# Moving the constants, the arena and the split inputs of a fused two-block decoder kernel to multiples of 1024 bytes in their partition

## The chip, the cores and the metric

The kernel runs on one core of one Trainium2 chip. The metric is the device time of one execution in microseconds (us). A core has TensorE (PE, whose weight loads are shown apart as PEld), VectorE (DVE), ScalarE (ACT), GpSimd (POOL), and SyncE (SP), which here issues all DMAs. Every tensor of the on-chip memory lies in 128 partitions; "the place" of a tensor is the byte in its partition at which it begins, and it is the same in all partitions.

## The reference

Two transformer blocks are applied to 256 tokens of width 1024, all in float32.

```python
def reference(x, mem, positions, ...):
    x = first_block(...)   # h = rms_norm(x); proj = h @ w_in; differential attention, indexed attention,
                           # gated sum @ w_out; memory attention; PEER feed-forward
    return second_block(...)   # layer 0: stick-breaking attention + RWKV7; layer 1: MLA
                               # each with a conv-GLU feed-forward and a gated per-layer embedding
```

In the PEER feed-forward each token picks, by product keys, 16 of 16,384 experts for each of 8 heads. The kernel computes it densely: 128 groups of 128 experts, of which each has a row of `peer_u` and a row of `peer_v`.

## The kernel before

All weights are streamed once through `ring`, four slots of 128 x 1024 float32 (512 KB), in the fixed order of `PLAN`. SP waits until a slot is free (`send`, L405) and issues the next DMA. Each slot is split in two halves of 128 x 512. ACT copies a half to `w_high` in the reduced format float32r (`split_high`, L453), DVE subtracts it from the original and writes the rest to `w_low` (`split_low`, L459), and both have four slots. The inputs of a product are split in the same manner into `a_high` and `a_low` (L1040, L1047, L1142 and L1147). A product of two float32 matrices is then made of three float32r matmuls in `three`:

```python
        (lh, ll), (rh, rl) = pairs
        self.nc.tensor.matmul(to, lh, rh, start=start, stop=False, **more)
        self.nc.tensor.matmul(to, lh, rl, start=False, stop=False, **more)
        return self.nc.tensor.matmul(to, ll, rh, start=False, stop=stop, **more)
```

For most products the weights (128 x 128) are stationary and the split inputs (128 x 256) are moving. These matmuls are L503, L504 and L505. Small products (sums of squares with the constant matrix `ones` at L907, L884 and L511, attention and the recurrence) are plain float32 matmuls; the profiler records each of those as two.

The tensors are laid out one behind the other, in the order in which `Kernel.__init__` (L290) names them; each begins at the next multiple of 32 bytes. Behind them come the tensors of a room (`room`, L321): an `arena` of so many floats, and then `a_high` and `a_low` (`pairs`, L333). A room is opened for a part of the program and closed behind it, and its place is used again. There are four rooms in turn:

- the first mixer, arena of 86 x 256 floats, 16 chunks of split inputs
- `peer` (L1953), arena of 128 x 256 floats. In the place of `a_high` and `a_low` (8 chunks) stand later `hot`, and then `s_high` and `s_low`, the split inputs of the products with `peer_v`
- `hybrid` (L2575), arena of `HYBRID_ROOM` floats, 11 chunks
- the rest of the second block, arena of 70 x 256 floats, 32 chunks

The products of `peer_u` (370 to 715 us) and of `peer_v` (833 to 1183 us) run mostly in a loop whose body handles four groups, so that the same instructions with the same places come round again and again. Semaphores order everything. Nothing in the order of the work depends on a place.

Of the kernel before, what the change touches and what calls it, by code (L numbers as in the profile page):

```python
# [29 lines left out]
P = 128  # L30
T = 256
TT = T // P
# [11 lines left out]
MEM_AT = 76 * T  # L44
POSITIONS_AT = 65 * T
PLE_AT = 30 * T
HYBRID_ROOM = 31488
AHEAD = 3
L = 64
SUB = 16  # L50
# [70 lines left out]
class Counter:  # L121


    def __init__(self, make):
        self.make, self.made, self.base, self.total = make, None, 0, 0
# [164 lines left out]
class Kernel:  # L290
    def __init__(self, nc, ctx, dram, out):
        self.nc, self.ctx, self.dram, self.out = nc, ctx, dram, out
        self.counters = {}
        sb = lambda name, shape, dt=F32: ctx.enter_context(nc.sbuf_tensor(name, shape, dt))
        self.x = sb("x", [P, DC, T])
        self.hn = sb("hn", [P, DC, T])
        self.ring = sb("ring", [P, RING, BLK * P])
        self.w_high = sb("w_high", [P, SLOTS, HALF * P], F32R)
        self.w_low = sb("w_low", [P, SLOTS, HALF * P], F32R)
        self.params = sb("params", [P, N_PARAMS])  # L300
        self.consts = sb("consts", [P, len(CONSTS), P])
        self.side = sb("side", [P, 6 * P])
        self.by_row = sb("by_row", [P, 2 * TT])
        self.small = sb("small", [P, 512])
        self.bank = [ctx.enter_context(nc.psum_tensor(f"bank{i}", [P, 512], F32)) for i in range(8)]
        self.landed = [ctx.enter_context(nc.semaphore(f"weights_landed{i}")) for i in range(RING)]
        self.high = ctx.enter_context(nc.semaphore("weights_high"))
        self.low = ctx.enter_context(nc.semaphore("weights_low"))
        self.used = ctx.enter_context(nc.semaphore("weights_used"))
        self.sent = 0  # L310
        self.split = 0
        self.taken = 0
        self.rooms = 0
        self.chains = {}
        self.x_landed = [ctx.enter_context(nc.semaphore(f"x_landed{i}")) for i in range(4)]
        self.consts_landed = ctx.enter_context(nc.semaphore("consts_landed"))
        self.fetched = Counter(
            lambda: ctx.enter_context(nc.semaphore("fetched")))
# [2259 lines left out]
    def hybrid(self):  # L2578
# [5 lines left out]
        def place(chunks, width=T):  # L2584
            at = free[0]
            free[0] += chunks * width
            assert free[0] <= HYBRID_ROOM - 2 * T
            return self.at(at, chunks, width)
# [772 lines left out]
def build(nc, dram, out):  # L3361
    with ExitStack() as ctx:
# [3 lines left out]
        k.peer()  # L3366
        with k.room(HYBRID_ROOM, DC + 3):
            out = k.hybrid()
# [139 lines left out]
```

How the kernel before makes its waits and increments, by code:

```python
        def link(ins):  # L357
            ins.then_inc(c.up(), 1)
            eng.wait_ge(c.sem, c.total)
# [46 lines left out]
    def send(self, sp, g, at, source, it=0, turn=0):  # L406
        if g >= RING:
            sp.wait_ge(self.low, it * (2 * turn) + 2 * (g - RING + 1))
        if self.wide(g):
            self.send_wide(sp, g, at)
            return
        if self.of("mla_uq", g):
            self.send_heads(sp, g, at)
            return
        sp.dma_start(self.ring[:, at, :], source).then_inc(self.landed[at], 16)
# [29 lines left out]
    def split_high(self, act, h, it=0, turn=0):  # L447
        g = h // 2
        act.wait_ge(self.landed[g % RING], it * (8 * turn // RING) + self.landings(g))
        if h >= SLOTS:
            act.wait_ge(self.used, it * turn + (h - SLOTS + 1))
        self.nc.scalar.activation(self.cut(h, self.w_high), self.raw(h), ACT.Copy)\
            .then_inc(self.high, 1)
# [1 line left out]
    def split_low(self, dve, h, it=0, turn=0):  # L456
        dve.wait_ge(self.high, it * turn + (h + 1))
        self.nc.vector.tensor_tensor(self.cut(h, self.w_low), self.raw(h),
                                     self.cut(h, self.w_high.bitcast(F32)), ALU.subtract)\
            .then_inc(self.low, 1)
# [22 lines left out]
    def block_of(self, pe, n):  # L484
        h = n // HALF
        if n % HALF == 0:
            pe.wait_ge(self.low, h + 1)
        at = slice((n % HALF) * P, (n % HALF + 1) * P)
        return self.w_high[:, h % SLOTS, at], self.w_low[:, h % SLOTS, at]
# [1031 lines left out]
        def bank_free(pe):  # L1522
            pe.wait_ge(kept.sem, kept.at(1))
```

## Time and profile before

| | |
|---|---|
| time, median of three runs | 2025.58 us |
| lowest and highest | 2023.09 and 2032.52 us |
| span of the profiled execution | 2021.6 us |
| PE busy | 1877.1 us, 93% |
| PEld, DVE, ACT busy | 1800.7, 1456.5 and 1242.6 us |
| DMA | 296.06 MB, 146 GB/s over the span |

The profiled execution's own time is known as its span alone; it lies 4.0 us below the median of the runs and 1.5 us below the lowest. The span runs from the first to the last instruction of the program. Busy times are sums over an engine's instructions. Matmuls overlap in the array and each is recorded with its full length, so a PE that is shown busy without a gap may still work at one pace or another; the pace is read from the starts.

### The profile page before, as it was taken

To read this page: it belongs to the slowest core of one execution; us is meant where nothing else is said; L and a number is where in the kernel's file an instruction comes from. 1 tells how busy PE (TensorE), PEld (TensorE's weight loads), DVE (VectorE), ACT (ScalarE), POOL (GpSimd) and SP (SyncE) were. 2 spreads that over 40 slices of the span, in tenths; PEclk is the share of its full clock that TensorE was granted. 3 is DMA by queue.
4 is the path that set the end of the run, shared out by engine and by line. 5 is a ranking of instruction groups with operands and counts; after the bars stand their busy time and mean duration, and the time that the engine had idled before them with its cause. 6 is when DMAs were issued, how large, how long until landed. Compare 5 with 4: busy or idle time off the path is not lost. (4 is left out here: it accounts for less than half of the span.)

```text
span 2021.6 us, 45016 instructions
## 1 busy us (share of the span) xinstructions
PE 1877.1 (93%) x16518; PEld 1800.7 (89%) x16518; DVE 1456.5 (72%) x3046; ACT 1242.6 (61%) x2420; POOL 0.2 (0%) x4
## 2 busy tenths in 40 slices
PE   8998988999999999999999989687999977999997
PEld 8887888999999976899999989587999976899996
DVE  7667667688985479766666667776888678578857
ACT  5454655777776789655555556733665555666555
POOL 0000000000000000000000000000000000000000
PEclk9999999999999999999999999798999989999998
DMA  6533344466655620266666646101665644166562
GB/s 208 158 97 105 118 143 136 132 194 193 179 186 175 186 84 0 84 194 190 196 191 193 193 139 199 52 3 56 184 196 173 192 126 136 34 190 189 176 198 76
DMA packets 102084, 296.06 MB, mean 146 GB/s; under 512 B 9539, under 2 KB 32454, under 8 KB 101830
## 3 DMA queue, kind: packets, MB, share of 16 engines
q1 hardware_dynamic: 101958, 294.35, 47.0%
q8 instruction: 83, 1.36, 0.3%
q14 instruction: 43, 0.35, 0.1%
HBM read 293.26 MB, written 1.05 MB: 146 GB/s over the span
## 5 line engine op out<-in xcount | busy, mean ns | idle before, releaser
L459 DVE TENSOR_TENSOR w_low<-ring,w_high 128x512 fp32r<-128x512 f32 x1102 | 743.2, 685 | 357.1 <-ACT w_high L453 349.2
L503 PE MATMUL bank<-a_high,w_high 128*128 128x256 f32 x3228 | 921.2, 285 | 74.3 <-DVE w_low L459 39.1
L504 PE MATMUL bank<-a_low,w_high 128*128 128x256 f32 x3228 | 907.5, 281 | 0.0
L505 PE MATMUL bank<-a_high,w_low 128*128 128x256 f32 x3228 | 907.4, 281 | 0.0
L453 ACT ACTIVATE w_high<-ring 128x512 fp32r<-128x512 f32 x1102 | 671.4, 624 | 375.3 <-PE bank L505 372.8
L503 PEld LDWEIGHTS bank<-a_high,w_high 128*128 128x128 f32 x3228 | 620.0, 192 | 90.0 <-DVE w_low L459 39.7
L504 PEld LDWEIGHTS bank<-a_low,w_high 128*128 128x128 f32 x3228 | 616.3, 191 | 0.4
L505 PEld LDWEIGHTS bank<-a_high,w_low 128*128 128x128 f32 x3228 | 616.7, 191 | 0.0
L503 PE MATMUL bank<-s_high,w_high 128*128 128x256 f32 x1024 | 283.5, 277 | 2.0 <-DVE s_low L2446 2.0
L504 PE MATMUL bank<-s_low,w_high 128*128 128x256 f32 x1024 | 283.3, 277 | 0.0
L505 PE MATMUL bank<-s_high,w_low 128*128 128x256 f32 x1024 | 283.3, 277 | 0.0
L503 PEld LDWEIGHTS bank<-s_high,w_high 128*128 128x128 f32 x1024 | 192.9, 188 | 2.2 <-DVE s_low L2446 2.2
L504 PEld LDWEIGHTS bank<-s_low,w_high 128*128 128x128 f32 x1024 | 193.0, 188 | 0.0
L505 PEld LDWEIGHTS bank<-s_high,w_low 128*128 128x128 f32 x1024 | 192.9, 188 | 0.0
L2329 PEld LDWEIGHTS bank<-hot 128*128 128x128 f32 x512 | 63.2, 194 | 28.6 <-issue 18.1
L2073 ACT ACTIVATE arena<-bank 128x256 f32 (+1 forms) x128 | 49.1, 384 | 58.0 <-PE bank L505 57.2
L2329 PE MATMUL bank<-hot 128*128 128x128 f32 x512 | 74.4, 290 | 9.8 <-ACT hot L2266 8.7
L1040 ACT ACTIVATE a_high<-x,params 128x256 fp32r<-128x256 f32 x72 | 31.9, 500 | 49.5 <-DVE x L1273 35.0
L2446 DVE TENSOR_TENSOR s_low<-arena,s_high 128x256 fp32r<-128x256 f32 x128 | 53.4, 418 | 0.8 <-ACT s_high L2426 0.8
L2300 DVE TENSOR_SCALAR hot<-consts,hn 128x128 f32<-128x128 f32 x192 | 53.2, 340 | 0.4 <-PEq L2023 0.4
L2426 ACT ACTIVATE s_high<-arena 128x256 fp32r (+1 forms) x128 | 51.5, 403 | 2.7 <-PEq L2243 2.7
L1047 ACT ACTIVATE a_high<-arena 128x256 fp32r<-128x256 f32 x87 | 30.5, 407 | 30.0 <-DVE arena L1333 12.7
(368 smaller groups left out, 1867.8 us busy)
## 6 DMA issues: line engine op xcount, KB each, us to landing
ring<-in_stream SPq DMA_DIRECT2D x273, 512.0 KB, 3.7
ring<-in_peer_u SPq DMA_DIRECT2D x128, 512.0 KB, 3.6
ring<-in_peer_v SPq DMA_DIRECT2D x128, 512.0 KB, 3.5
ring<-in_stream SPq DMA_DIRECT2D x32, 256.0 KB, 3.3
ring<-in_stream SPq DMA_DIRECT2D x12, 192.0 KB, 2.7
x<-in_x SPq DMA_DIRECT2D x4, 256.0 KB, 6.3
arena<-in_mem SPq DMA_DIRECT2D x1, 1024.0 KB, 11.0
out<-x SPq DMA_DIRECT2D x4, 256.0 KB, 2.6
```

What stands on the lines that cost most here:

```text
L453: self.nc.scalar.activation(self.cut(h, self.w_high), self.raw(h), ACT.Copy)\
L459: self.nc.vector.tensor_tensor(self.cut(h, self.w_low), self.raw(h), self.cut(h, self.w_high.bitcast(F32)), ALU.subtract)\
L503: self.nc.tensor.matmul(to, lh, rh, start=start, stop=False, **more)
L504: self.nc.tensor.matmul(to, lh, rl, start=False, stop=False, **more)
L505: return self.nc.tensor.matmul(to, ll, rh, start=False, stop=stop, **more)
L1040: ins = nc.scalar.activation(self.a_high[:, to, :], source.source[:, c, :], ACT.Copy, scale=self.param(source.gain, c))
L1047: ins = nc.scalar.activation(self.a_high[:, to, :], source[:, c, :], ACT.Copy)
L2073: nc.scalar.activation(to, self.bank[k % 4][:, 0:T], ACT.Gelu)\
L2300: ins = nc.vector.tensor_scalar(hot[:, 1, b, i, :], iota, one(1), one(2), ALU.is_equal, ALU.mult)
L2329: ins = nc.tensor.matmul(self.bank[b][:, i * P:(i + 1) * P], hot[:, 0, b, i, :], hot[:, 1, b, i, :], start=True, stop=True)
L2426: nc.scalar.activation(s_high[:, k % SIDES, :], self.arena[:, bass.ds(it * (RING * T) + k * T, T)], ACT.Copy).then_inc(cut[0].sem, 1)
L2446: nc.vector.tensor_tensor(s_low[:, k % SIDES, :], self.arena[:, bass.ds(it * (RING * T) + k * T, T)], s_high[:, k % SIDES, :].bitcast(F32) ...
```

## The change

One tensor is made larger and moved, and one room is made smaller. `by_row` (16 bytes, four per-partition factors) stood between `side` and `small`. It is now the beginning of `filled` (480 bytes), which stands between `params` and `consts`.

```diff
-HYBRID_ROOM = 31488
+HYBRID_ROOM = 31232
...
         self.params = sb("params", [P, N_PARAMS])
+        self.filled = sb("filled", [P, 120])
+        self.by_row = self.filled[:, 0:2 * TT]
         self.consts = sb("consts", [P, len(CONSTS), P])
         self.side = sb("side", [P, 6 * P])
-        self.by_row = sb("by_row", [P, 2 * TT])
         self.small = sb("small", [P, 512])
```

`HYBRID_ROOM` loses 256 floats, 1024 bytes, which makes up for the bytes that the gap adds; what `hybrid` places in it (at most `HYBRID_ROOM - 512` floats, asserted at L2587) still fits, and the last 512 floats of the arena, its `scratch`, move down with its end.

The places of the built programs, in bytes from the start of the partition:

| tensor | before | after | remainder by 1024, before and after |
|---|---|---|---|
| x, hn, ring, w_high, w_low, params | 16512, 24704, 32896, 49280, 57472, 65664 | the same | 128 and 128 |
| consts | 67104 | 67584 | 544 and 0 |
| side | 75296 | 75776 | 544 and 0 |
| small | 78400 | 78848 | 576 and 0 |
| arena, every room | 80448 | 80896 | 576 and 0 |
| a_high, a_low, first room | 168512, 184896 | 168960, 185344 | 576 and 0 |
| a_high, a_low, peer | 211520, 219712 | 211968, 220160 | 576 and 0 |
| hot and s_high; s_low | 211520; 215616 | 211968; 216064 | 576 and 0 |
| a_high, a_low, hybrid | 206400, 217664 | 205824, 217088 | 576 and 0 |
| a_high, a_low, last room | 152128, 184896 | 152576, 185344 | 576 and 0 |

The instructions of every engine and of SP stand in the same order in both programs, with the same shapes, numbers and waits; where the profile will name `by_row` it will name `filled`, and lines behind L301 are one higher.

## Rows read from the trace of the kernel before

**Rows 1.** The page, part 1: busy us (share of the span) and instructions.

```profile
PE 1877.1 (93%) x16518; PEld 1800.7 (89%) x16518; DVE 1456.5 (72%) x3046; ACT 1242.6 (61%) x2420; POOL 0.2 (0%) x4
```

**Rows 2.** Groups by line: busy us, mean ns | idle before, releaser.

```profile
L503 PE MATMUL bank<-a_high,w_high 128*128 128x256 f32 x3228 | 921.2, 285 | 74.3 <-DVE w_low L459 39.1 <-DVE a_low L1147 15.8 <-DVE a_low L1142 10.8
...
L459 DVE TENSOR_TENSOR w_low<-ring,w_high 128x512 fp32r<-128x512 f32 x1088 | 737.9, 688 | 356.0 <-ACT w_high L453 348.3
L453 ACT ACTIVATE w_high<-ring 128x512 fp32r<-128x512 f32 x1088 | 666.3, 627 | 368.7 <-PE bank L505 366.2
...
L505 PE MATMUL bank<-s_high,w_low 128*128 128x256 f32 x1024 | 283.3, 277 | 0.0
```

**Rows 3.** Windows: length; PE, PEld, DVE, ACT, POOL busy (x starts); PEclk, DMA, GB/s.

```profile
370.00:521.00 151.00, 151.00 (x1335) 151.00 (x1334) 130.00 (x435) 117.20 (x195) 0.00 (x0) 1.00 0.63 191
...
838.00:1182.00 344.00, 344.00 (x3038) 344.00 (x3037) 217.00 (x378) 198.14 (x379) 0.00 (x0) 1.00 0.62 192
...
1918.00:1971.00 53.00, 53.00 (x470) 53.00 (x469) 31.52 (x51) 26.68 (x47) 0.00 (x0) 1.00 0.65 197
```

**Rows 4.** Windows of five other stretches, the same columns.

```profile
617.00:649.00 32.00, 32.00 (x273) 32.00 (x273) 15.11 (x25) 20.68 (x38) 0.00 (x0) 1.00 0.59 182
652.00:714.00 62.00, 62.00 (x528) 62.00 (x528) 31.07 (x48) 47.21 (x80) 0.00 (x0) 1.00 0.62 192
1456.00:1550.00 94.00, 94.00 (x801) 94.00 (x799) 77.97 (x144) 57.77 (x107) 0.00 (x0) 1.00 0.62 186
1763.00:1783.00 20.00, 20.00 (x172) 20.00 (x171) 13.44 (x24) 10.45 (x20) 0.00 (x0) 1.00 0.56 173
1806.00:1912.00 106.00, 106.00 (x902) 106.00 (x902) 88.14 (x163) 65.04 (x121) 0.00 (x0) 1.00 0.60 186
```

**Rows 5.** Windows of PE alone: length, busy (x), PEclk, DMA, GB/s.

```profile
233.00:253.00 20.00, 20.00 (x173) 1.00 0.56 171
...
1973.00:1985.00 12.00, 12.00 (x104) 1.00 0.58 176
```

**Rows 6.** Timeline of PE in the peer_u loop at 500 us: start, length.

```profile
500.08 0.28 PE L503 MATMUL bank<-a_high,w_high 128*128 128x256 f32 x1
...
500.42 0.28 PE L503 MATMUL bank<-a_high,w_high 128*128 128x256 f32 x1
```

**Rows 7.** Timeline of PE in the same loop at 680 us.

```profile
679.85 0.28 PE L503 MATMUL bank<-a_high,w_high 128*128 128x256 f32 x1
...
680.20 0.28 PE L503 MATMUL bank<-a_high,w_high 128*128 128x256 f32 x1
```

**Rows 8.** Timeline of PE at 616.7 us, where the pace changes.

```profile
616.81 0.39 PE L503 MATMUL bank<-a_high,w_high 128*128 128x256 f32 x1 [0.67 <-DVE w_low L459]
617.04 0.28 PE L504 MATMUL bank<-a_low,w_high 128*128 128x256 f32 x1
...
617.27 0.28 PE L503 MATMUL bank<-a_high,w_high 128*128 128x256 f32 x1
```

**Rows 9.** Source views of L907, L884 and L511: min/median/max ns, first and last start.

```profile
L907 PE MATMUL bank<-hn,consts x50: 377/379/380, 26.5 to 1987.6; 128*128 128x256 f32 x50
...
L884 PE MATMUL bank<-arena,consts x36: 377/379/380, 33.9 to 87.7; 128*128 128x256 f32 x36
...
L511 PE MATMUL bank<-consts x50: 377/379/634, 295.8 to 1724.0; 128*128 128x256 f32 x50
```

**Rows 10.** Groups by line of DVE: busy us, mean ns | idle before.

```profile
L1171 DVE TENSOR_TENSOR hn<-hn 128x512 f32<-128x512 f32 x28 | 19.2, 684 | 0.0
...
L1207 DVE TENSOR_TENSOR arena<-arena 128x512 f32<-128x512 f32 x11 | 7.6, 692 | 0.4
```

**Rows 11.** DMA issues: count, KB each, median us to landing.

```profile
ring<-in_stream SPq DMA_DIRECT2D x273, 512.0 KB, 3.7
...
arena<-in_mem SPq DMA_DIRECT2D x1, 1024.0 KB, 11.0
```

**Rows 12.** Waits: us, times, longest.

```profile
ACT w_high L453 <- PE bank L505: 372.8, 572, 2.6
...
ACT L1040 <- DMA x<-in_x: 6.8, 1, 6.8
```

## The prediction

> **What bounds the kernel now.** I read the page's busy times first, then the groups by line, then windows of long stretches, and last the starts of single matmuls. PE is busy for 1877.1 of 2021.6 us [rows 1]; POOL does nothing. In the groups, ACT idles 366.2 us before its weight split because it waits for PE to free a slot of the split weights, and DVE idles 348.3 us because it waits for ACT [rows 2]; the list of waits says the same, 572 waits of at most 2.6 us [rows 12]. PE itself idles 74.3 us before L503, the line that starts most products. So PE sets the pace, the splitters wait for it, and the weights' DMAs, 3.7 us to landing [rows 11], are issued when the splitters have freed a slot. Half the time comes from one kind of instruction: L503, L504 and L505 with 128 x 256 moving, 3 x 3228 with `a_` inputs and 3 x 1024 with `s_` inputs, 12,756 in all [rows 2].
>
> The length of a record says little, since matmuls overlap. The pace is what counts, and the reader is to see two paces. In long stretches where PE never pauses and the granted clock is 1.00 (the 2.4 GHz level), 344 us hold 3038 matmuls, 151 us hold 1335 and 53 us hold 470 [rows 3]. A count includes the two that began before the stretch, so the pitch is 344 / 3036 = 113.3 ns, and 113.3 and 113.2 in the others. In seven other stretches, also without a pause and at clock 1.00, the counts are 273 in 32 us, 528 in 62, 801 in 94, 172 in 20 and 902 in 106 [rows 4], and 173 in 20 and 104 in 12 [rows 5]: 346 us for 2939 matmuls, 117.7 ns. Single starts show it too: three matmuls take 0.34 us at 500 us [rows 6] and 0.35 us at 680 us [rows 7], in the same loop with the same tensors in the same places. The slow pace begins where PE restarts after a wait [rows 8] and then lasts for hundreds of matmuls. So for the weight products there is a second, slower pace of the pair "load the next weights, stream the inputs", 4.4 ns per matmul dearer, into which PE falls at some restarts.
>
> **The change part by part.** It adds no instruction, removes none, and moves none in any queue, SP's included. What changes is where tensors begin. Each of its effects is a difference in how long an instruction takes.
>
> (1) The moving operand of the weight products goes from remainder 576 to 0 by 1024, while the stationary weights stay at 128 (or 640, by the 512-byte block). No row of before has `a_high` at another remainder, so I bound it. Nearest is the same 128 x 256 shape with a constant matrix beside it: with `hn`, which begins at remainder 128, L907 takes 377/379/380 ns; with the arena, at 576, L884 takes 377/379/380 ns [rows 9]. Two remainders, no difference in minimum, median or maximum. Those are plain float32 matmuls, whose stationary side is `consts`, but they read on-chip memory in the same shape. I take 0. The bounds from other rows are the two paces: all matmuls of the seven slow stretches at the fast pace gives 2939 x 4.4 ns = 13 us less; all of the three long fast stretches (1333 + 3036 + 468 = 4837) at the slow pace gives 21 us more, and every one of the 12,756 - 2939 = 9817 others gives at most 43 us more, since waits and half-clock stretches hide part of that.
>
> (2) The constants go from remainder 544, which is no multiple of 64, to 0. L511 has constants on both sides and a median of 379 ns, the same as L907 and L884, which have them on one side only [rows 9]. Its maximum of 634 is a matmul at the low clock level or behind a pause. So the price is 0; if the one or two ns that rounding hides were real, 144 records (50 + 36 + 50 and L907's eight others) make under 0.3 us.
>
> (3) DVE and ACT read and write arena, `small` and split inputs. DVE's 128 x 512 addition-like operation takes 684 ns with `hn` (128) on all sides and 692 ns with the arena (576) on all sides [rows 10]; if the arena's remainder were the cause, DVE would gain at most 8 ns on each. Both engines wait for PE, 366.2 and 348.3 us, so this hides, except where DVE's chain between two products holds PE: PE idles 74.3 us before L503 [rows 2], and 8 / 692 of that is 0.9 us. I take 0 and keep -1 us for the range.
>
> (4) `by_row` moves; its four factors per partition are read as scales. Nothing there depends on bulk reads: 0. The 1024 bytes less in `hybrid` leave out unused space: 0.
>
> (5) DMAs. The weights' slots stay at 128 by 1024, so the loads that run all through the kernel land as they did. What changes is the landing of the constants, the memory tokens, keys and a few small loads, once each; the largest takes 11.0 us and lands while PE works, and the first thing on the start's path is the load of `x`, 6.8 us of waiting [rows 11, 12], whose place is unchanged: 0.
>
> The sum is 0 against the profiled span of 2021.6 us. The median of the runs lies 4.0 us above that span, and I forecast it unchanged, **2025.6 us**. The time by itself moves, though: the three runs spread over 9.4 us, and the seven slow stretches show a reason, restarts that fall to one pace or the other. If the restarts fall otherwise in the changed kernel without any cause in the places, a few us either way follow; one long stretch of 106 us changing pace is 902 x 4.4 ns = 4 us. I give that +-8 us. About 10 us (0.5%) is what a measurement of this kernel can tell from no change.
>
> **A rule to weigh.** The rows show one instruction, with one set of places and clock 1.00, at two paces that differ by 3.9% [rows 3, 4]; something that PE reads or shares costs it those 4.4 ns in one state and not in the other. The Trainium skill, page "SBUF — State Buffer", section on the two separate sides, says that on the engine side only the port pair shared by VectorE and GpSimd causes contention, and that TensorE never waits for anyone. By that rule the place can't matter and the sum is exactly 0, with neither of the first two rivals below possible. The two paces don't fit well with it, which is why I keep the rivals.
>
> A second rule speaks for a small gain. The page "DMA: Bandwidth & Descriptors", section on how a descriptor splits, says that a transfer that doesn't start at a multiple of 256 bytes costs one more transaction for each descriptor. By it the 8 KB rows of the memory tokens would need 32 instead of 33, an estimate of 0.3 us on 11.0, beside other work, while the weights' 512 KB slots gain nothing since the change leaves them at 128. The sum by it stays 0.
>
> **The rivals.**
>
> *The slow pace goes away (faster).* The weight load and the moving read may hinder each other depending on the distance of their places. The change makes that distance 896 instead of 448 by 1024. For: two paces exist, one set of places gives both, so the state is a matter of phase, and a distance shifts a phase. Against: within a stretch the weights' remainder alternates between 128 and 640 and the pace doesn't, so 512 bytes of distance are worth nothing; and L907 and L884, whose distances to the constants differ by those same 448 bytes, take the same time [rows 9]. Time: 2025.6 - 13 = 2012.6 us, or about 2008 if the many short slow stretches that I didn't sum go too. It decides (over 10 us) once three quarters of the slow matmuls change. Chance 0.22, in it a small part for larger gains by a shorter pitch altogether.
>
> *The slow pace takes over (slower).* The same mechanism with the other sign: at the new distance more restarts fall to the slow pace, above all in the `peer_v` loop, which is fast from 838 to 1182 us [rows 3]. That loop alone costs 3036 x 4.4 = 13 us, and all three long fast stretches 21 us: 2039 to 2047 us. It decides once 10 / 0.0044, some 2300 of the fast matmuls, turn slow, so the `peer_v` loop is enough. For: that loop has never been slow in this trace though it is the longest stretch, which may be owed to its places. Against: the `peer_u` loop uses `a_high` at the place that `s_high` has, and has both paces [rows 3, 4]. Chance 0.16.
>
> *The change doesn't do what it says.* Here the places are known from the built program, so it does, apart from the tensors up to `params`, which aren't aligned at all. If places matter only where all operands are aligned, the result is no change: part of the forecast.
>
> **How the numbers follow.** No change, within 10 us, has 0.62; faster 0.22; slower 0.16. The range reaches down to 2010 (the fast rival's 2012.6 with some scatter; 0.05 lies below, where the pitch itself falls or all short stretches go too) and up to 2042 (the `peer_v` loop slow, and a little more; 0.09 lies above). The likeliest case alone would be 2018 to 2034.
>
> **What would show it.** If right: the pitch in 838 to 1182 us is still 113.3 ns, slow stretches are still there at 117.7 ns and hold 2500 to 5000 matmuls, L907 and L884 still 379, L1171 and L1207 within a few ns of 684 and 692. If the fast rival holds, every window without a pause has 8.8 matmuls per us. If the slow one holds, windows of the `peer_v` loop have 8.5. A pitch that is neither 113.3 nor 117.7 would make my account of the price wrong, whatever the total.

## The result and the profile after

The changed kernel takes **2064.95 us** (median of five runs), the kernel before 2025.58 us; the ratio is 1.0174, 95% interval 1.0138 to 1.021. Measured a second time, beside other kernels, it took 2063.14 us (2061.8 to 2064.49) against 2028.8 us, ratio 1.0157, interval 1.0092 to 1.0222. Ratios here and below are estimates over all comparable runs of both kernels, not quotients of the two medians. I had forecast 2025.6 us with a range of 2010 to 2042, so the result lies outside it, on the side to which I gave 0.16.

One of the five runs, the one profiled first, took 3499.76 us (its matmuls in 860 to 1160 us lay 233 ns apart at a granted clock of 1.00, and the clock was 0.55 from 2600 to 3400 us; why is not known), and it is left out of the ratio; the other four took 2061.01 to 2065.24 us. The rows of after are those of the second measurement ("again"), whose profiled span is 2060.0 us: 38.4 us more than the span before.

The page of the changed kernel, part 1, answers to [rows 1]:

```profile
PE 1916.9 (93%) x16518; PEld 1839.6 (89%) x16518; DVE 1458.6 (71%) x3046; ACT 1245.6 (60%) x2420; POOL 0.2 (0%) x4
```

PE's busy time has grown by 39.8 us with the same 16,518 matmuls. DVE and ACT are 2 and 3 us up. In the groups by line of the changed kernel (busy us, mean ns | idle before, releaser), which answer to [rows 2]:

```profile
L504 PE MATMUL bank<-a_high,w_high 128*128 128x256 f32 x3228 | 929.1, 288 | 71.5 <-DVE w_low L460 36.7 <-DVE a_low L1148 15.6 <-DVE a_low L1143 9.7
...
L460 DVE TENSOR_TENSOR w_low<-ring,w_high 128x512 fp32r<-128x512 f32 x1088 | 739.4, 689 | 385.8 <-ACT w_high L454 377.0
L454 ACT ACTIVATE w_high<-ring 128x512 fp32r<-128x512 f32 x1088 | 667.0, 627 | 401.2 <-PE bank L506 399.9
...
L506 PE MATMUL bank<-s_high,w_low 128*128 128x256 f32 x1024 | 288.1, 281 | 0.0
```

PE waits no longer than before (71.5 us against 74.3). The splitters take the same time for each half (689 and 627 ns against 688 and 627) and wait longer for PE (399.9 us against 366.2). So nothing new is waited for; PE itself is slower. The windows of two stretches of [rows 3], the same columns:

```profile
370.00:521.00 151.00, 151.00 (x1275) 151.00 (x1274) 124.37 (x424) 115.26 (x190) 0.00 (x0) 1.00 0.59 181
838.00:1182.00 344.00, 341.74 (x2870) 340.13 (x2868) 209.97 (x372) 190.50 (x367) 0.00 (x0) 1.00 0.57 178
```

In the first, 1275 - 2 = 1273 matmuls in 151 us are 118.6 ns each, where 1333 had 113.3. The second now begins ahead of the `peer_v` loop. A window that lies inside that loop in every kernel of this study, 860 to 1160 us, shows PE alone (length, busy, clock, DMA, GB/s), first before the change:

```profile
860.00:1160.00 300.00, 300.00 (x2650) 1.00 0.62 193
```

and then in the changed kernel:

```profile
860.00:1160.00 300.00, 300.00 (x2531) 1.00 0.59 184
```

That is 300 / 2648 = 113.3 ns before and 300 / 2529 = 118.6 ns after. The timeline of PE in this loop of the changed kernel, start and length in us:

```profile
999.77 0.28 PE L504 MATMUL bank<-s_high,w_high 128*128 128x256 f32 x1
999.89 0.28 PE L505 MATMUL bank<-s_low,w_high 128*128 128x256 f32 x1
...
1001.08 0.28 PE L506 MATMUL bank<-s_high,w_low 128*128 128x256 f32 x1
```

From the first to the last of these rows eleven matmuls start in 1.31 us, 0.12 us apart, with no wait between them.

Where the 38.4 us went can be read from the source view of L503 before and L504 after (min/median/max ns, first and last start). Before:

```profile
L503 PE MATMUL bank<-s_high,w_high x1024: 276/276/497, 833.0 to 1182.5; 128*128 128x256 f32 x171
```

After:

```profile
L504 PE MATMUL bank<-s_high,w_high x1024: 279/281/386, 847.0 to 1211.2; 128*128 128x256 f32 x171
```

The loop begins 14.0 us later, takes 364.2 instead of 349.5 us (14.7 more), and what follows it takes 848.8 instead of 839.1 us (9.7 more). The loss is spread over all weight products. Where the pitch before was 113.3 ns a matmul now costs 5.3 ns more, and where it was 117.7 ns only 0.9 ns. Taken over all unbroken stretches of more than 60 weight products at full clock (some 10,600 of the 12,756), the mean pitch is 114.84 ns before and 118.67 ns after, and 10,600 times the difference of 3.83 ns is 41 us. By this estimate the pitch accounts for the whole 38.4 us.

The kinds of instruction on which my zero rested have not changed. Not only their lengths are the same, their starts are too: four matmuls of L884 in a row take 1.02 us before and 1.03 us after, about 215 ns from start to start. First before the change:

```profile
33.86 1.02 PE L884 MATMUL bank<-arena,consts 128*128 128x256 f32 x4
```

and then after it:

```profile
34.14 1.03 PE L885 MATMUL bank<-arena,consts 128*128 128x256 f32 x4
```

The source views of the changed kernel, L908 and L885, answer to [rows 9]:

```profile
L908 PE MATMUL bank<-hn,consts x50: 377/379/381, 26.7 to 2026.1; 128*128 128x256 f32 x50
...
L885 PE MATMUL bank<-arena,consts x36: 377/379/381, 34.1 to 88.6; 128*128 128x256 f32 x36
```

And its groups of DVE answer to [rows 10]:

```profile
L1172 DVE TENSOR_TENSOR hn<-hn 128x512 f32<-128x512 f32 x28 | 19.2, 686 | 0.0
...
L1208 DVE TENSOR_TENSOR arena<-arena 128x512 f32<-128x512 f32 x11 | 7.6, 692 | 0.4
```

### The profile page after: what moved, and what is told of

It reads as the page before. It is cut to its first block and busy times, and to the rows that moved or that the text cites. A ratio compares the mean times of both kernels' runs of the same rounds, so it can differ in the third digit from the quotient of the medians.

```text
span 3498.0 us, 45016 instructions
## 1 busy us (share of the span) xinstructions
PE 3420.5 (98%) x16518; PEld 3287.0 (94%) x16518; DVE 1486.9 (43%) x3046; ACT 1267.8 (36%) x2420; POOL 0.2 (0%) x4
## 5 line engine op out<-in xcount | busy, mean ns | idle before, releaser
L504 PE MATMUL bank<-a_high,w_high 128*128 128x256 f32 x3228 | 1346.3, 417 | 31.8 <-DVE a_low L1148 10.2
L505 PE MATMUL bank<-a_low,w_high 128*128 128x256 f32 x3228 | 1337.2, 414 | 0.0
L506 PE MATMUL bank<-a_high,w_low 128*128 128x256 f32 x3228 | 1336.3, 414 | 0.0
L504 PEld LDWEIGHTS bank<-a_high,w_high 128*128 128x128 f32 x3228 | 1048.0, 325 | 44.9 <-issue 31.6
L505 PEld LDWEIGHTS bank<-a_low,w_high 128*128 128x128 f32 x3228 | 1052.0, 326 | 2.3 <-issue 1.2
L506 PEld LDWEIGHTS bank<-a_high,w_low 128*128 128x128 f32 x3228 | 1051.6, 326 | 0.1
L504 PE MATMUL bank<-s_high,w_high 128*128 128x256 f32 x1024 | 448.9, 438 | 2.0 <-DVE s_low L2447 2.0
L506 PE MATMUL bank<-s_high,w_low 128*128 128x256 f32 x1024 | 448.9, 438 | 0.0
L504 PEld LDWEIGHTS bank<-s_high,w_high 128*128 128x128 f32 x1024 | 364.7, 356 | 2.3 <-DVE s_low L2447 2.3
L505 PEld LDWEIGHTS bank<-s_low,w_high 128*128 128x128 f32 x1024 | 364.9, 356 | 0.0
L506 PEld LDWEIGHTS bank<-s_high,w_low 128*128 128x128 f32 x1024 | 364.8, 356 | 0.0
L2074 ACT ACT_TABLE_LOAD x31 | 39.8, 1283 | 67.3 <-PE bank L506 67.3
```

The lines of the kernel that those rows point to most:

```text
L2074: nc.scalar.activation(to, self.bank[k % 4][:, 0:T], ACT.Gelu)\
```

## The experiments

All of them move tensors and change nothing else; every one issues the instructions of the kernel before. "The distance" is the place of the split inputs (`a_high`, `a_low`, `s_high`, `s_low`) less that of the weights (`w_high`, `w_low`), by 256. It is one number for all four pairs and for all chunks, because blocks of weights are 512 bytes apart and all other steps are multiples of 1024. It is 192 before and 128 in the changed kernel.

### Which tensors

**again.** The changed kernel itself.

> The changed kernel once more, for a profile at the usual clock. The pace theory (at the new places more restarts fall to the slow pitch of 117.7 ns): about 2060 us, stretches without a pause at 8.5 matmuls per us nearly everywhere, the peer_v loop among them, 3.5% longer there than before. The rival that something else became slower (loads, VectorE, ScalarE): pitches of 113.3 ns as before in the peer_v loop, and new idle time of TensorE before L504. A third possibility is a pitch that before did not have at all.

Measured: 2063.14 us, pitch 118.6 ns, shown above. The slow side is right, but not by the pace that I had expected: 118.6 is the third possibility.

**a_only.** Only the split inputs (and `hot`, which shares their place) move.

```diff
 # the kernel before
-HYBRID_ROOM = 31488
+HYBRID_ROOM = 31232
...
-        with self.nc.sbuf_tensor(f"arena{self.rooms}", [P, floats], F32) as self.arena:
+        with self.nc.sbuf_tensor(f"arena{self.rooms}", [P, floats], F32) as self.arena, \
+                self.nc.sbuf_tensor(f"gap2_{self.rooms}", [P, 112], F32):
```

> The kernel before, with a gap of 448 bytes ahead of the split inputs of each room and of hot, s_high and s_low, and nothing else moved: the split inputs begin at remainder 0, constants, small and arena stay at 544 and 576. If the place of the split inputs (their distance to the weights or their own multiple) is the cause, this is as slow as the changed kernel, about 2060 us. If the constants or the arena are, it is as before, 2025 us.

Measured: 2067.12 us, ratio 1.0181 (1.0109 to 1.0252), as slow as the changed kernel. The window of PE in the `peer_v` loop:

```profile
860.00:1160.00 300.00, 300.00 (x2530) 1.00 0.59 184
```

**c_only.** All but the split inputs stay at their new places.

```diff
 # the changed kernel
-        with self.nc.sbuf_tensor(f"arena{self.rooms}", [P, floats], F32) as self.arena:
+        with self.nc.sbuf_tensor(f"arena{self.rooms}", [P, floats], F32) as self.arena, \
+                self.nc.sbuf_tensor(f"gap2_{self.rooms}", [P, 144], F32):
```

> The changed kernel, with a gap of 576 bytes ahead of the split inputs: constants, side, small and arena begin at multiples of 1024, the split inputs at remainder 576 as before. If the split inputs are the cause: 2025 us. If the constants or the arena are: 2060 us.

Measured: 2031.57 us, ratio 0.9997 (0.9958 to 1.0035). The two together settle it: the split inputs carry the whole loss, and constants, `side`, `small` and arena at multiples of 1024 are worth nothing that can be measured.

### The place or the distance

**all_moved.** Everything from `x` on moves by 448 bytes.

```diff
 # the kernel before
-HYBRID_ROOM = 31488
+HYBRID_ROOM = 31232
...
+        self.gap0 = sb("gap0", [P, 112])
         self.x = sb("x", [P, DC, T])
```

> The kernel before, with one gap of 448 bytes ahead of x: every tensor is 448 bytes further, the split inputs begin at remainder 0 by 1024 as in the changed kernel, and every distance is the one of before. The theory of the distance to the weights: 2025 us, with both pitches. The theory that the multiple of 1024 of the split inputs itself costs: about 2060 us.

Measured: 2024.89 us, ratio 0.9982 (0.9952 to 1.0012), with the split inputs at multiples of 1024. Its window:

```profile
860.00:1160.00 300.00, 300.00 (x2650) 1.00 0.61 192
```

So it is not where the split inputs begin, but how far they are from something else. The place of the weights alone isn't the cause either: they moved by the same 448 bytes.

**weights_64.** From the changed kernel, only `w_high`, `w_low` and `params` move.

```diff
 # the changed kernel
+        self.gap = sb("gap", [P, 16])
         self.w_high = sb("w_high", [P, SLOTS, HALF * P], F32R)
...
-        self.filled = sb("filled", [P, 120])
+        self.filled = sb("filled", [P, 104])
```

> The changed kernel with a gap of 64 bytes ahead of w_high, and filled shorter by 64 bytes: constants, side, small, arena and all split inputs stay exactly where the changed kernel has them, at multiples of 1024, and only w_high, w_low and params are 64 bytes further. The distance of the split inputs to the weights is 832 by 1024, 64 by 128. If that distance by 128 is the cause: 2025 us, and pitches of 113.3 and 117.7 ns. If the places of the change itself cost: 2063 us.

Measured: 2056.49 us, ratio 1.0108 (1.0029 to 1.0188). A miss for the time that the rule of 128 bytes gave, and yet a change: the pitch in the loop is the slower of the two of before, 300 / 2547 = 117.8 ns.

```profile
860.00:1160.00 300.00, 300.00 (x2549) 1.00 0.60 185
```

**weights_192.** The same with 192 bytes, which makes the distance 192 as before.

```diff
 # the changed kernel
+        self.gap = sb("gap", [P, 48])
         self.w_high = sb("w_high", [P, SLOTS, HALF * P], F32R)
...
-        self.filled = sb("filled", [P, 120])
+        self.filled = sb("filled", [P, 72])
```

> The changed kernel with a gap of 192 bytes ahead of w_high, and filled shorter by 192 bytes: everything from consts on stays at the multiples of 1024 of the changed kernel, w_high, w_low and params are 192 bytes further, and the distance is 704, 192 by 256 as in before. The theory of a period of 256 bytes: 2020 to 2035 us, with a pitch of 113.3 ns in the peer_v loop. If the multiples of 1024 cost anything besides the distance, it stays at 2055 us or more.

Measured: 2028.69 us against 2028.08, ratio 1.0003 (0.9968 to 1.0037).

```profile
860.00:1160.00 300.00, 300.00 (x2650) 1.00 0.62 192
```

This is the changed kernel with every tensor of the change at its multiple of 1024, and the loss is gone. The split inputs keep the distance of the changed kernel to `ring`, constants and arena here; only the one to the weights (and `params`, which no matmul reads) is restored. So it is the pair of the two operands of the product.

### Which distances are good

A gap ahead of the split inputs was made 32 to 384 bytes long in the kernel before, by the edit of a_only with another length (`[P, gap / 4]`), and `HYBRID_ROOM` as in the kernel before.

> The kernel before with a gap of 64 bytes ahead of the split inputs: their distance to the stationary weights is 512 by 1024 (448 before, 896 in the changed kernel), that is 0 by 512, 0 by 256 and 0 by 128. If the distance by 128 decides (64 in before, 0 in the changed kernel), this has the third pitch of 118.7 ns and some 2063 us. If the distance by 256 or 512 decides it is a new value and either pitch can come. If only whole multiples of 1024 of the split inputs' own place cost, 2025 us.

> Gap of 128 bytes: distance 576 by 1024, 64 by 512, 64 by 256, 64 by 128. If the distance by 128 decides: as before, 113.3 and 117.7 ns, 2025 us. If the one by 256 decides (192 in before, 128 in the changed kernel) it is open.

> Gap of 192 bytes: distance 640 by 1024, 128 by 512, 128 by 256, 0 by 128. If the distance by 128 or by 256 decides: 118.7 ns, 2063 us. If the one by 512 decides (448 in before, 384 in the changed kernel) it is open.

> Gap of 256 bytes: distance 704 by 1024, 192 by 512, 192 by 256, 64 by 128. If the distance by 128 or by 256 decides: as before, 113.3 and 117.7 ns, 2025 us. If that by 512 decides it is open.

> The kernel before with a gap of 320 bytes ahead of the split inputs: distance 256 by 512, 0 by 256 and 0 by 128. By the rule of 128 bytes it is slow, some 2065 to 2075 us. If 256 bytes are the period of the finer pattern, it has the single pitch of 120.0 ns that a gap of 64 bytes has; if it is 512, some other pitch.

> Gap of 384 bytes: distance 320 by 512, 64 by 256, 64 by 128. By the rule of 128 bytes: pitches of 113.3 and 117.7 ns and no other, 2020 to 2055 us according to where the restarts fall.

> Gap of 32 bytes: the split inputs and the weights are an odd multiple of 32 bytes apart (480 by 512, 96 by 128). If units of 64 bytes are read, each moving read of 1024 bytes touches one unit more and the pitch is at least that of the slow state, 2045 us or more. If 32 bytes of distance only shift the phase, a pitch at or below 113.3 ns could come, 2010 us.

> Gap of 224 bytes ahead of the split inputs: distance 160 by 256, between 128 (118.7 to 120 ns) and 192 (113.3 or 117.7 ns). If distance 192 is the one good value: 2045 to 2070 us, like the other odd multiple of 32 (118.3 ns). If the good zone is centred lower, pitches at or below 113.3 ns and below 2020 us.

> Gap of 96 bytes: distance 32 by 256, between 0 (120.0 ns) and 64 (117.8 ns). If 192 is the one good value: 118 to 120 ns, 2055 to 2077 us. Any stretch at 113.3 ns or less is against it.

> Gap of 160 bytes: distance 96 by 256, between 64 (117.8 ns) and 128 (118.7 to 120 ns). If 192 is the one good value: 117 to 120 ns, 2050 to 2077 us. Any stretch at 113.3 ns or less is against it.

Two more put them 16 bytes to either side of 192, which needs a tensor that is used from its byte 16 on:

```diff
 # in pairs, and likewise for s_high and s_low
-        with self.nc.sbuf_tensor(f"a_high{self.rooms}", shape, F32R) as self.a_high, \
-                self.nc.sbuf_tensor(f"a_low{self.rooms}", shape, F32R) as self.a_low:
+        with self.nc.sbuf_tensor(f"a_both{self.rooms}", [P, 4 + 2 * chunks * T], F32R) as both:
+            high, low = (both[:, 4 + i * chunks * T:4 + (i + 1) * chunks * T] for i in range(2))
+            self.a_high = high.rearrange("p (c t) -> p c t", t=T)
+            self.a_low = low.rearrange("p (c t) -> p c t", t=T)
             yield
```

> The kernel before, with each pair of split inputs in one tensor that is 16 bytes longer, used from its byte 16 on: they are 16 bytes further, distance 208 by 256, between 192 (113.3 or 117.7 ns) and 224 (118.3 ns). If reads go by units of 32 bytes or more, an input that begins in the middle of one costs at least a further unit and the pitch is 115 ns or more, 2040 to 2075 us. If only the phase counts and 192 isn't its best value, a pitch below 113.3 ns or fewer slow stretches, below 2020 us.

> The same with a gap of 224 bytes besides, 240 in all: distance 176 by 256, between 160 and 192. By the same two readings: 115 ns or more and 2040 to 2075 us, or below 113.3 ns and below 2020 us.

All results in one table. The pitch is 300 us over the count of the window 860 to 1160 less 2, in the one profiled execution of each kernel. Times without a star are medians of repeated runs, with a star one run each. The kernel before, measured beside them, had medians of 2028 to 2029 us in the three larger groups and a spread of 2020 to 2050 us over single runs; gap_64, gap_128, gap_192 and gap_256 had one run of it beside them, of 2042.3 us. So a single time says less than the pitch beside it.

| distance by 256 | kernels | pitch in the peer_v loop, ns | time, us |
|---|---|---|---|
| 0 | gap_64, gap_320 | 120.0, 120.0 | 2074.7*, 2077.1* |
| 32 | gap_96 | 116.7 | 2050.4* |
| 64 | gap_128, gap_384, weights_64 | 117.8, 117.7, 117.8 | 2054.6*, 2058.0*, 2056.5 |
| 96 | gap_160 | 120.0 | 2078.9* |
| 128 | again, a_only, gap_192 | 118.6, 118.7, 120.0 | 2063.1, 2067.1, 2067.6* |
| 160 | gap_224 | 117.3 | 2067.2* |
| 176 | gap_240 | 119.2 | 2075.5* |
| 192 | before, all_moved, c_only, weights_192, gap_256 | 113.3 in all five | 2025.6, 2024.9, 2031.6, 2028.7, 2027.2* |
| 208 | gap_16 | 119.1 | 2065.7* |
| 224 | gap_32 | 118.3 | 2066.5* |

Rows of the windows of four of them, in this order: gap_64, gap_96, gap_128 and gap_256.

```profile
860.00:1160.00 300.00, 300.00 (x2502) 1.00 0.59 182
```

```profile
860.00:1160.00 300.00, 300.00 (x2573) 1.00 0.60 187
```

```profile
860.00:1160.00 300.00, 300.00 (x2549) 1.00 0.59 186
```

```profile
860.00:1160.00 300.00, 300.00 (x2650) 1.00 0.63 193
```

The reader is to see three things. Distances that differ by 256 bytes behave alike: 0 and 0 from gaps of 64 and 320, 64 from 128 and 384, 192 from 0 and 256. A period of 128 bytes doesn't fit: 0 differs from 128, 32 from 160 and 96 from 224. By the time and by the pitch in this loop one of the ten distances tried is good, 192, and the kernel before had it. Every other took 22 us or more over the 2028 us of the kernel before. For gap_96 (2050.4 us in its one run) the pitch has to carry that, since the slowest single run of the kernel before took 2050.0 us. And none of the ten gives a faster kernel.

Several expectations were missed in size. gap_96 was to be at 118 to 120 ns and 2055 to 2077 us and came out at 116.7 ns and 2050.4 us. gap_64 and gap_192 were to be at 118.7 ns in the loop by the rule of 128 bytes and had 120.0. gap_160, gap_240, gap_320 and gap_384 took up to 3 us more than their ranges allowed.

The distance doesn't settle everything. A distance has one, two or three paces, and with few exceptions the pace changes only where PE restarts after a wait. At 128 the `peer_v` loop has 118.6 ns in the changed kernel and 120.0 in gap_192, but gap_192 itself has both: its `peer_u` loop (165 us / 1376 = 119.9 ns) and a later stretch (107 us / 903 = 118.5 ns):

```profile
373.00:538.00 165.00, 165.00 (x1378) 1.00 0.60 182
1847.00:1954.00 107.00, 107.00 (x905) 1.00 0.62 184
```

At 208 the `peer_u` loop of gap_16 has 154 us / 1320 = 116.7 ns, where its `peer_v` loop has 119.1:

```profile
375.00:529.00 154.00, 154.00 (x1322) 1.00 0.63 190
```

And at 64 the two paces are those of 192. gap_128 runs a late stretch at 52 us / 459 = 113.3 ns:

```profile
1951.00:2003.00 52.00, 52.00 (x461) 1.00 0.65 192
```

So the rule of 128 bytes fell for the times of gap_128 and weights_64, which it had put at 2025 us, and of gap_384, which it had put at 2055 us at most, but not for the set of their paces. What sets 64 and 192 apart is how often a restart falls to the fast pace. Among the weight products in unbroken stretches of more than 60 at full clock, 54 to 79% are at the fast pace in the five kernels with 192, and 1 to 6% in the three with 64. At the other eight distances no stretch is that fast.

At 192 both paces occur in one kernel. In weights_192 the windows of PE show the fast one in the `peer_u` and `peer_v` loops and the slow one (58 us / 492 = 117.9 ns) later:

```profile
370.00:520.00 150.00, 150.00 (x1326) 1.00 0.63 193
830.00:1174.00 344.00, 344.00 (x3037) 1.00 0.63 192
1484.00:1542.00 58.00, 58.00 (x494) 1.00 0.62 185
```

In all_moved, with the same distance, the `peer_u` loop has the slow one, from 372 to 520 us (148 us / 1257 = 117.7 ns), and the `peer_v` loop has not:

```profile
372.00:520.00 148.00, 148.00 (x1259) 1.00 0.61 185
850.00:1170.00 320.00, 320.00 (x2826) 1.00 0.61 193
```

## Why the prediction was wrong

- **What bounds the kernel** held. PE sets the pace, the splitters wait for it, and the whole loss is in PE's pitch. The two paces of [rows 3] and [rows 4] were real and were the clue. "Half the time" for the 12,756 weight products was too low: at 113.3 ns each they take 1445 us, 71% of the span.
- **Term 1, the moving operand at another remainder, "I take 0"**, is the step that failed. It measured +38 us between the profiled spans. Its nearest rows, L907 and L884, are plain float32 matmuls at 379 ns each (L884's constant is a rotation and not `ones`, and L511 multiplies the identity by zeros, so only L907 is a sum of squares). They stayed at 379 ns in the changed kernel though both changed their distance to the constants, by 256 from 96 to 128 and from 32 to 0. So at these four distances their pace doesn't answer to places, and they could not speak for the float32r products. They were the nearest row in shape and the wrong one in kind.
- **The bound of that term** was too low as well. I reckoned with the slow pace of 117.7 ns as the worst, +21 us for the three long stretches and +43 at most. The changed kernel has 118.6 ns in the `peer_v` loop, 5.3 ns more than 113.3, and 120.0 ns exists too, at the same distance in gap_192. The result would have been inside the +43 that I wrote down and left out of the range, but only in size: no long stretch of the changed kernel runs at the 117.7 ns from which the +43 was worked out.
- **"512 bytes of distance are worth nothing"** was right, and the conclusion from it was not: with a period of 256 bytes the alternation of the weights by 512 can show nothing of the distance.
- **The slower rival** was right in mechanism and place (the distance of the two operands, first of all the `peer_v` loop, whose speed I noted "may be owed to its places") and low in price: 2039 to 2047 us against 2065. The counter-argument, that `a_high` has both paces at the place that `s_high` has, is true and proves little: 192 is a distance at which both paces exist, and 128 one at which neither was seen.
- **Terms 2 to 5** held. c_only, which has all of them and not term 1, has a ratio of 0.9997 (0.9958 to 1.0035). L1172 stands at 686 ns and L1208 at 692. The estimated gain of 0.3 us on the memory tokens can't be seen: they took 11.0 us from issue to landing before and 11.1 in the changed kernel, and 11.0 to 11.7 over six kernels without regard to the multiple of 256.
- **The rule of the Trainium skill** on the page "SBUF — State Buffer", that TensorE never waits for anyone, would have made the sum exactly 0, and the runs go against it as a rule for the time: TensorE's own products take 113.3 to 120.0 ns by the distance of their two operands. They don't contradict it as a rule on other engines, since c_only and weights_192, which move tensors against those that the other engines use, cost nothing. Of TensorE's own two reads the same section of the Trainium skill says, in its table of bandwidths, that weight loads have a second, independent read port; the pitches by distance show that the pair of operands is not without effect on the time, though no run here shows where the time goes.
- **What would make it wrong**, as I named it: a pitch that is neither 113.3 nor 117.7 ns. That is what came.

That the two reads collide in something that repeats every 256 bytes is my reading of the table, and not shown by itself: the loads of the next stationary operand weren't timed alone. Not settled is what sends a restart into one pace or another. The spread of the kernel before (2020 to 2050 us over all its runs here) probably comes from it: of the five profiled kernels at distance 192 the one with the fewest products at the slow pace (weights_192, 21%) has the shortest span, 2014.8 us, and the two with the most (gap_256 and all_moved, 43 and 46%) the longest, 2025.4 and 2023.0 us. No slow run of one and the same kernel was profiled to show it.

## What to carry to other kernels

Where products of float32r like these (128 x 128 stationary, 128 x 256 moving) follow each other without a pause, the pitch depends on the distance between the places of the stationary and the moving tensors, by 256 bytes; in three kernels (all_moved, c_only, weights_192) the multiple of 1024 at which tensors begin was worth nothing. A tensor that is added or lengthened anywhere between the two can change the pitch of all these products, unless it shifts them by a multiple of 256 bytes. So a change of layout is to be timed as a change of its own, and a kernel's good distance (here 192) is kept with a gap when the layout changes. To see the pitch, count matmuls in a window in which TensorE never pauses at a granted clock of 1.00. Busy time says 100% at every pitch, and the length of a record changes by only a few ns (a median of 276 in the `peer_v` loop before and 281 after), far less plainly than the count.

## What the runs showed that was not expected

- One identical sequence of matmuls, without a pause and at clock 1.00, has pitches between 113.3 and 120.0 ns according to the distance and, at six of the ten distances, to the last restart, 5.9% apart; 16 bytes of distance take it from 113.3 to 119.1 in the `peer_v` loop (gap_16).
- At the distance of 0 the pitch is one single value, 120.0 ns, in both loops of both kernels; at 128, in the changed kernel's loops, single starts in the trace follow each other at 115 to 122 ns, which the mean of 118.6 hides.
- Plain float32 matmuls of the same shape (L907, L884) don't show it: about 215 ns from start to start before and after.
- The distances 64 and 192 have the same two paces, 113.3 and 117.7 ns, and differ in how often a restart takes the fast one.
